# Four output projections stream their 256 tokens in another order of 64- or 128-byte pieces

## The chip, the core and the metric

The kernel runs on one core of one Trainium2 chip. The metric is the device time of one execution in microseconds (us). Three runs of the kernel before took 2223.46, 2226.57 and 2227.17 us; the median is 2226.57.

## What is computed

Three layers of a sequence model are computed for 256 tokens of width 2048, in fp32: an mLSTM and convolution mixer with a gated feed-forward layer, then a gated linear attention (GLA) mixer, then a latent attention (MLA) mixer. Cut to what matters here, four dense layers end the parts of it:

```
h = h + merged @ w_out                          # "wout":   2048 -> 2048
h = h + (silu(gate) * val) @ w_down             # "wdown":  5504 -> 2048
y = (o * silu(gate)) @ l0_gla_w_out             # "glaout": 2048 -> 2048
y = (o * silu(gate)) @ l1_mla_w_out             # "mlaout": 2048 -> 2048
x = x + rms_norm(y, g_post)                     # after glaout and mlaout
```

Before wdown stands the up projection (`hn @ w_up`, 2048 to 2 times 5504), a root-mean-square norm ahead of it.

## The kernel before, in words

Activations lie transposed in the on-chip memory (SBUF): 128 features on the partitions, the 256 tokens along each partition (`T = 256`, four bytes each, so 1024 bytes of a partition to a tile of features). Weights come from DRAM as one stream in the order of their use, in units of 128 x 1024 numbers, four units in a ring. ScalarE rounds each unit to `w_hi` (line 921), VectorE makes the rest `w_lo` (line 1337); each activation is held as a `hi` and a `lo` part too. A product of a 128 x 128 block of weights with a tile of tokens is then three matmuls in `tile` (lines 554 to 556): `w_hi` with `hi`, `w_hi` with `lo`, `w_lo` with `hi`. In each the block of weights is loaded into the array (the stationary operand, row "PEld" of the profile), and the 256 tokens stream past it (the moving operand) and are added in 256 columns of a PSUM bank, `acc0` or `acc1`. `feature_tile` does this for 16 blocks, that is 48 matmuls and two units of weights; wout, glaout and mlaout are 16 such tiles each (768 matmuls each), wdown is 16 tiles of 43 blocks (2064 matmuls), the up projection 86 tiles (4128 matmuls).

`token_tiles` (lines 596 to 598) has the roles the other way round: tokens are stationary, 256 or 512 columns of the weights stream. Sums over features (norms, softmax) and the small products of attention are plain fp32 matmuls, each of which the chip runs as two passes. One of these stands inside the up projection: `norm_sum` (line 605) is issued between the two units of its first tile.

The order on TensorE is fixed by the program: the stages follow each other in one instruction stream, the fixed loops of each stage wait only on semaphores for the next unit (`lo_ready`), for the bank (`acc_taken`) and for their inputs. VectorE and ScalarE read `acc` after the last matmul of a tile, columns 0 to 255 in their natural order.

Where the operands lie is set by the layout: `apart` (192 bytes) stands between the weights and `n_hi`, and the shared area starts 64 bytes past a multiple of 256:

```
LINE = 256
apart = sb("apart", [P, LINE // 4 * 3 // 4])
arena_start = -(-(nc.sbuf_base - LINE // 4) // LINE) * LINE + LINE // 4
```

With this layout every unit of `w_hi` and `w_lo` starts 128 bytes past a multiple of 256, and every tile of a moving operand of `tile` (`n_hi`, `mg_hi`, `f_hi`, `og_hi`, `mo_hi`, `c_hi` and their `lo` parts) starts 64 bytes past one.

Of the kernel before, what the change touches and what calls it, by code (L numbers as in the profile page):

```python
# [19 lines left out]
T = 256  # L20
D = 2048
KT = D // P
# [7 lines left out]
F_TILES = D_FF // P  # L30
# [5 lines left out]
RING = 4  # L36
FREE = 1
LINE = 256


PHASES = [
# [26 lines left out]
def program(nc, x_in, stream_in, params_in, v_bias_in, gk2_in, positions_in, out):  # L68
# [26 lines left out]
    with ctx:  # L95
        def sb(name, shape, dt=fp32):
            return ctx.enter_context(nc.sbuf_tensor(name, shape, dt))
# [15 lines left out]
        w_hi = sb("w_hi", [P, RING, UNIT], fp32r)  # L113
        w_lo = sb("w_lo", [P, RING, UNIT], fp32r)
        apart = sb("apart", [P, LINE // 4 * 3 // 4])
        n_hi = sb("n_hi", [P, KT, T], fp32r)
# [16 lines left out]

        arena_start = -(-(nc.sbuf_base - LINE // 4) // LINE) * LINE + LINE // 4
        arena_end = nc.sbuf_usable_end
# [14 lines left out]
        a = Arena(arena_start)  # L150
# [12 lines left out]
        a = Arena(mixer_temps)  # L163
# [45 lines left out]
        a = Arena(arena_start)  # L209
        f_hi = a.place("f_hi", [P, F_TILES, T], fp32r)  # L210
        f_lo = a.place("f_lo", [P, F_TILES, T], fp32r)
# [11 lines left out]
        a = Arena(arena_start)  # L223
# [24 lines left out]
        a = Arena(y_at)  # L248
        log_a = a.place("log_a", [P, G_HEADS, 2 * T])
        rank_rows = a.place("rank_rows", [32, T])  # L250
        a = Arena((arena_end - 4 * T) // 32 * 32)
        out_rstd = a.place("out_rstd", [P, T])
        a = Arena(y_at + 4 * G_HEADS * 2 * T + 4 * T)
        gk2 = a.place("gk2", [G_RANK + 1, G_HEADS * G_DK])
        a = Arena(y_at)
# [7 lines left out]
        a = Arena(arena_start)  # L263
# [4 lines left out]
        c_hi = a.place("c_hi", [P, 2 * A_TILES, T], fp32r)  # L268
        c_lo = a.place("c_lo", [P, 2 * A_TILES, T], fp32r)
# [14 lines left out]
        a = Arena(y2_at)  # L284
# [5 lines left out]
        a = Arena(y2_at)  # L290
# [7 lines left out]
        a = Arena(arena_start + 4 * 2 * C_TILES * T)  # L298
# [238 lines left out]
        def _(pe):  # L537
            def unit(name, i, j):

                u, s, _ = unit_of(name, i, j)  # L540
                pe.wait_ge(lo_ready, u + 1)
                return s

            def bank(b, name, i, j):

                uses = count(1 + b, name, i, j)
                if i is not None or uses:
                    pe.wait_ge(acc_taken[b], FREE + uses)
                return acc[b]

            def tile(out, s, c, hi, lo, k, first, last):

                wc = slice(c * P, (c + 1) * P)
                nc.tensor.matmul(out, w_hi[:, s, wc], hi[:, k, :], start=first, stop=False)  # L554
                nc.tensor.matmul(out, w_hi[:, s, wc], lo[:, k, :], start=False, stop=False)  # L555
                return nc.tensor.matmul(out, w_lo[:, s, wc], hi[:, k, :], start=False, stop=last)  # L556

            def feature_tile(name, i, j, b, use, hi, lo, wait_act=None, ready=(), unscaled=None, between=None):

                o = bank(b, name, i, use)[:, 0:T]  # L560
                for n in range(2):
                    s = unit(name, i, j + n)
                    for c in range(8):
                        if wait_act is not None and c % 4 == 0:

                            four = wait_act * KT // 4 + 2 * n + c // 4 + 1
                            pe.wait_ge(act_ready, 3 * four)
                            pe.wait_ge(act_ready_dve, four)
                        if unscaled is not None:

                            pe.wait_ge(xlo_ready, UNSCALED[unscaled] * KT + 8 * n + c + 1)
                        if c % 4 == 0:

                            for signal, per in ready:
                                pe.wait_ge(signal, FREE + (8 * n + c + 4) // per)
                        last = tile(o, s, c, hi, lo, 8 * n + c, n + c == 0, 8 * n + c == KT - 1)
                    last.then_inc(unit_done, 1)
                    if n == 0 and between is not None:
                        between()
# [40 lines left out]


            feature_tile("gates", None, 0, 0, 0, n_hi, n_lo, wait_act=0)

            def mix(i):
                feature_tile("mix", i, 0, 1, 0, n_hi, n_lo)
                feature_tile("mix", i, 2, 0, 0, n_hi, n_lo)


# [43 lines left out]
            with pe.Fori(0, KT // 2) as i:  # L672
                for m in range(2):
                    feature_tile("merge", i, 6 * m, 1, 2 * m, n_hi, n_lo)
                    feature_tile("merge", i, 6 * m + 2, 0, 2 * m, n_hi, n_lo)
                    for n, (hi, lo) in enumerate(((hm_hi, hm_lo), (yc_hi, yc_lo))):

                        if n == 0:
                            pe.wait_ge(hmlo_ready, FREE + M_HEADS)
                        else:  # L680
                            pe.wait_ge(yclo_ready, FREE + 2 * M_HEADS)
                        o = bank(1 - n, "merge", i, 2 * m + 1)[:, 0:T]
                        s = unit("merge", i, 6 * m + 4 + n)
                        for c in range(8):
                            last = tile(o, s, c, hi, lo, c, c == 0, c == 7)
                        last.then_inc(unit_done, 1)

            with pe.Fori(0, KT // 2) as i:
# [14 lines left out]
            with pe.Fori(0, KT // 2) as i:  # L703
                for m in range(2):
                    o = bank(1 - m, "wdown", i, 0)[:, 0:T]
                    for n in range(6):
                        s = unit("wdown", i, 6 * m + n)
                        pe.wait_ge(flo_ready, FREE + min(8 * n + 8, F_TILES))
                        for k in range(8 * n, min(8 * n + 8, F_TILES)):
                            last = tile(o, s, k - 8 * n, f_hi, f_lo, k, k == 0, k == F_TILES - 1)  # L710
                        last.then_inc(unit_done, 1)


# [112 lines left out]
            def pair_tile(i, j, b, use, k0):  # L826


                pe.wait_ge(c_ready, k0 + A_TILES)
                o = bank(b, "mla", i, use)  # L830
                s = unit("mla", i, j)
                for c in range(8):
                    m, k = divmod(c, A_TILES)
                    last = tile(o[:, m * T:(m + 1) * T], s, c, c_hi, c_lo, k0 + k, k == 0,
                                k == A_TILES - 1)
                return last

# [30 lines left out]
            with pe.Fori(0, A_HEADS // 4) as i:  # L868
                for n in range(2):
                    pair_tile(i, 2 * n, 0, n, 0).then_inc(unit_done, 1)  # L870
                    pair_tile(i, 2 * n + 1, 1, n, A_TILES).then_inc(unit_done, 1)

                last = pair_tile(i, 4, 0, 2, 0)
                unit("mla", i, 5)
                last.then_inc(unit_done, 2)
# [1361 lines left out]
```

## Time and profile before

| | |
|---|---|
| median of 3 runs | 2226.57 us |
| the profiled execution's own time | 2226.45 us |
| its span, first to last instruction | 2224.7 us |
| TensorE matmul busy | 2145.7 us (96%), 17596 instructions |
| TensorE weight load busy | 2104.9 us (95%) |
| VectorE, ScalarE, GpSimd busy | 59%, 52%, 13% |
| mean granted TensorE clock | 0.985 of 2.4 GHz |
| DMA | 177 GB/s mean, 49% of the 16 engines |

The profile is of one execution. Its matmuls are pipelined and their ends are modelled: one of 256 columns is shown with 276 or 281 ns while the next starts some 115 ns later. So the busy share says little of how fast TensorE goes; the distance from one start to the next (the pitch, below) says it. It is read from the first and the last start of a group and its count, or from the number of matmuls in a stretch. A matmul of line 554, 555 or 556 counts once each.

### The profile page before, as it was taken

The page shows a single profiled execution, that of the slowest core. Times are in us where ns is not written, and L with a number is a line of the kernel's source. Part 1 is how long each engine was busy: PE and PEld are TensorE (multiplying, and loading weights), DVE is VectorE, ACT ScalarE, POOL GpSimd, SP SyncE. Part 2 cuts the span into 40 slices and gives each one's busy share as a digit, 9 for nine tenths or more (in the row PEclk, how much of TensorE's full clock was granted, in tenths as well). Part 3 has the DMA queues.
Part 4 walks back from the last instruction along what each step waited for, and adds up shares of the span by engine and source line. Part 5 has one row for each costly group of instructions (what it writes and reads, how often), then busy time and mean ns, then how long its engine had stood idle before and what let it go on. Part 6 is the DMA issues. An engine that isn't in the chain of part 4 may idle for free.

```text
span 2224.7 us, 46503 instructions
## 1 busy us (share of the span) xinstructions
PE 2145.7 (96%) x17596; PEld 2104.9 (95%) x17596; DVE 1312.7 (59%) x1641; ACT 1158.4 (52%) x1544; POOL 283.3 (13%) x325
## 2 busy tenths in 40 slices
PE   5999999999999999999999999999999979999996
PEld 5999999999999999999999999999998969899996
DVE  5655664544557666666765545655665465755644
ACT  5444545555546555555554444644554445656542
POOL 2000000010110111111111100001010123111112
PEclk8999999999999999999999999999999989999998
DMA  4454545555555555555545555445444434444453
GB/s 150 172 183 174 189 163 198 194 187 202 189 189 192 186 188 189 187 183 181 187 186 208 193 218 212 146 178 190 171 169 170 171 131 147 157 151 152 155 183 113
DMA packets 54927, 393.83 MB, mean 177 GB/s; under 512 B 6097, under 2 KB 6225, under 8 KB 7522
## 3 DMA queue, kind: packets, MB, share of 16 engines
q1 hardware_dynamic: 54432, 392.19, 49.2%
q10 hardware_dynamic: 450, 1.02, 0.1%
q8 instruction: 31, 0.51, 0.1%
q14 instruction: 14, 0.11, 0.0%
HBM read 391.09 MB, written 2.10 MB: 177 GB/s over the span
## 4 chain that ended last, share of the span: by engine, by line
PE 80%; issue 13%; POOL 3%; DVE 2%; ACT 2%; DMA 0%; POOLq 0%; DVEq 0%; ACTq 0%
PE acc L554 23%; PE acc L555 23%; PE acc L556 23%; PE tok L596 2%; PE tok L598 2%; PE tok L597 2%; POOL n_lo L1927 1%; POOL sumsq_g L1918 1%; PE att L614 1%; POOL x L1940 0%; POOL probs L2080 0%; DVE rstd L1345 0%; POOL probs L2077 0%; PE att L788 0%; PE att L864 0%
## 5 line engine op out<-in xcount | busy, mean ns | idle before, releaser
L1337 DVE TENSOR_TENSOR w_lo<-raw,w_hi 128x1024 fp32r<-128x1024 f32 x740 | 907.0, 1239 | 728.2 <-ACT w_hi L921 726.1
L921 ACT ACTIVATE w_hi<-raw 128x1024 fp32r<-128x1024 f32 x740 | 770.0, 1056 | 594.7 <-PE acc L556 363.5
L554 PE MATMUL acc<-n_hi,w_hi 128*128 128x256 f32 x3488 | 986.7, 283 | 26.8 <-POOL n_lo L1927 19.4
L555 PE MATMUL acc<-n_lo,w_hi 128*128 128x256 f32 x3488 | 979.6, 281 | 0.0
L556 PE MATMUL acc<-n_hi,w_lo 128*128 128x256 f32 x3488 | 979.4, 281 | 0.0
L554 PEld LDWEIGHTS acc<-n_hi,w_hi 128*128 128x128 f32 x3488 | 668.7, 192 | 30.1 <-issue 20.2
L555 PEld LDWEIGHTS acc<-n_lo,w_hi 128*128 128x128 f32 x3488 | 662.0, 190 | 0.5
L556 PEld LDWEIGHTS acc<-n_hi,w_lo 128*128 128x128 f32 x3488 | 660.8, 189 | 0.0
L555 PE MATMUL acc<-f_lo,w_hi 128*128 128x256 f32 x688 | 193.5, 281 | 0.0
L556 PE MATMUL acc<-f_hi,w_lo 128*128 128x256 f32 x688 | 193.5, 281 | 0.0
L554 PE MATMUL acc<-f_hi,w_hi 128*128 128x256 f32 x688 | 193.5, 281 | 0.0
L554 PEld LDWEIGHTS acc<-f_hi,w_hi 128*128 128x128 f32 x688 | 132.2, 192 | 0.0
L555 PEld LDWEIGHTS acc<-f_lo,w_hi 128*128 128x128 f32 x688 | 129.2, 188 | 0.0
L556 PEld LDWEIGHTS acc<-f_hi,w_lo 128*128 128x128 f32 x688 | 129.2, 188 | 0.0
L1994 POOL TENSOR_TENSOR f_lo<-f_act,f_hi 128x256 f32 x43 | 57.6, 1340 | 432.3 <-ACT f_hi L1100 432.3
L1916 POOL TENSOR_TENSOR sumsq<-sumsq,square 128x256 f32<-128x256 f32 x64 | 47.3, 739 | 444.4 <-ACT square L930 227.5
L596 PE MATMUL tok<-w_hi,n_hi 128*128 128x256 f32 (+1 forms) x256 | 87.6, 342 | 0.0
L598 PE MATMUL tok<-w_hi,n_lo 128*128 128x256 f32 (+1 forms) x256 | 87.2, 341 | 0.0
L597 PE MATMUL tok<-w_lo,n_hi 128*128 128x256 f32 (+1 forms) x256 | 87.2, 341 | 0.0
L554 PE MATMUL acc<-og_hi,w_hi 128*128 128x256 f32 x256 | 72.1, 282 | 3.1 <-DVE og_lo L1730 3.1
L554 PE MATMUL acc<-mo_hi,w_hi 128*128 128x256 f32 x256 | 72.1, 282 | 0.0
L555 PE MATMUL acc<-mo_lo,w_hi 128*128 128x256 f32 x256 | 72.0, 281 | 0.0
(313 smaller groups left out, 2950.8 us busy)
## 6 DMA issues: line engine op xcount, KB each, us to landing
raw<-stream_in SPq DMA_DIRECT2D x370, 1024.0 KB, 4.8
x<-x_in SPq DMA_DIRECT2D x4, 512.0 KB, 7.4
out<-x SPq DMA_DIRECT2D x4, 512.0 KB, 2.6
v_bias<-v_bias_in ACTq DMA_DIRECT2D x1, 512.0 KB, 8.9
par<-params_in ACTq DMA_DIRECT2D x1, 287.0 KB, 5.5
pos_i<-positions_in ACTq DMA_DIRECT2D x1, 128.0 KB, 6.8
gk<-gk_in ACTq DMA_DIRECT2D x1, 68.0 KB
```

What stands on the lines that cost most here:

```text
L554: nc.tensor.matmul(out, w_hi[:, s, wc], hi[:, k, :], start=first, stop=False)
L555: nc.tensor.matmul(out, w_hi[:, s, wc], lo[:, k, :], start=False, stop=False)
L556: return nc.tensor.matmul(out, w_lo[:, s, wc], hi[:, k, :], start=False, stop=last)
L596: nc.tensor.matmul(o, hi[:, k0 + k, tt], w_hi[:, s, wc], start=k == 0, stop=False)
L597: nc.tensor.matmul(o, hi[:, k0 + k, tt], w_lo[:, s, wc], start=False, stop=False)
L598: last = nc.tensor.matmul(o, lo[:, k0 + k, tt], w_hi[:, s, wc], start=False, stop=k == n_k - 1)
L614: last = nc.tensor.matmul(att[3][:, 0:T], ones[:, :], squares_all[:, k, :], start=k == 0, stop=k == KT - 1)
L921: nc.scalar.activation(w_hi[:, s, :], raw[:, s, :], ACT.Copy).then_inc(hi_ready, 1)
L1337: nc.vector.tensor_tensor(w_lo[:, s, :], raw[:, s, :], w_hi[:, s, :].bitcast(fp32), ALU.subtract).then_inc(lo_ready, 1)
L1916: ins = gp.tensor_tensor(sumsq[:, :], sumsq[:, :], square[:, m, :], ALU.add)
L1918: ins = gp.tensor_tensor(sumsq_g[:, :], sumsq_g[:, :], square_g[:, m, :], ALU.add)
L1994: gp.tensor_tensor(f_lo[:, i, :], f_act[:, :], f_hi[:, i, :].bitcast(fp32), ALU.subtract)\
```

## The change

`tile` is given the name of its stage. For the four output stages it views the token axis of the moving operand and of the PSUM output through the same rearrangement, so each token's result still lands in its own column, while tokens are visited in another order. In units of 64-byte pieces (16 tokens), numbered 0 to 15 along the tile, the orders are:

- wout: 0 2 4 6 8 10 12 14, then 1 3 5 7 9 11 13 15
- wdown: 0 8 1 9 2 10 3 11 4 12 5 13 6 14 7 15
- glaout: 0 1, 8 9, 2 3, 10 11, 4 5, 12 13, 6 7, 14 15
- mlaout: 0 1, 4 5, 8 9, 12 13, then 2 3, 6 7, 10 11, 14 15

All other stages keep the natural order. No instruction is added, removed or moved on any engine; the matmuls of the four stages have one more level in two of their access patterns. Nothing that VectorE, ScalarE, GpSimd or the DMA queues do is changed.

```
+STREAMED = {"wout": "p (a b e) -> p b a e", "wdown": "p (b a e) -> p a b e",
+            "glaout": "p (b a e) -> p a b e", "mlaout": "p (a b e) -> p b a e"}
+STREAM_RUN = {"wout": 16, "wdown": 16, "glaout": 32, "mlaout": 32}
...
-            def tile(out, s, c, hi, lo, k, first, last):
+            def streamed(name, t):
+
+                if name not in STREAMED:
+                    return t
+                return t.rearrange(STREAMED[name], b=2, e=STREAM_RUN[name])
+
+            def tile(name, out, s, c, hi, lo, k, first, last):
 
                 wc = slice(c * P, (c + 1) * P)
-                nc.tensor.matmul(out, w_hi[:, s, wc], hi[:, k, :], start=first, stop=False)
-                nc.tensor.matmul(out, w_hi[:, s, wc], lo[:, k, :], start=False, stop=False)
-                return nc.tensor.matmul(out, w_lo[:, s, wc], hi[:, k, :], start=False, stop=last)
+                out, high, low = streamed(name, out), streamed(name, hi[:, k, :]), streamed(name, lo[:, k, :])
+                nc.tensor.matmul(out, w_hi[:, s, wc], high, start=first, stop=False)
+                nc.tensor.matmul(out, w_hi[:, s, wc], low, start=False, stop=False)
+                return nc.tensor.matmul(out, w_lo[:, s, wc], high, start=False, stop=last)
...
-                        last = tile(o, s, c, hi, lo, 8 * n + c, n + c == 0, 8 * n + c == KT - 1)
+                        last = tile(name, o, s, c, hi, lo, 8 * n + c, n + c == 0, 8 * n + c == KT - 1)
...
-                            last = tile(o, s, k - 8 * n, f_hi, f_lo, k, k == 0, k == F_TILES - 1)
+                            last = tile("wdown", o, s, k - 8 * n, f_hi, f_lo, k, k == 0, k == F_TILES - 1)
```

## Rows read from the trace of the kernel before

**Rows 1.** The page: busy time of the engines, share of the span, instructions
```profile
PE 2145.7 (96%) x17596; PEld 2104.9 (95%) x17596; DVE 1312.7 (59%) x1641; ACT 1158.4 (52%) x1544; POOL 283.3 (13%) x325
```
**Rows 2.** Longest waits of TensorE: in total, times, longest, us
```profile
PE acc L554 <- POOL n_lo L1927: 19.4, 5, 7.7
...
PE acc L554 <- DVE og_lo L1730: 3.1, 1, 3.1
```
**Rows 3.** Matmuls by operand: duration ns min/median/max, first and last start, us
```profile
L554 PE MATMUL acc<-mg_hi,w_hi x256: 275/276/277, 591.5 to 678.2; 128*128 128x256 f32 x128
...
L554 PE MATMUL acc<-f_hi,w_hi x688: 280/281/282, 1165.1 to 1407.8; 128*128 128x256 f32 x172
...
L554 PE MATMUL acc<-og_hi,w_hi x256: 280/281/356, 1713.7 to 1807.1; 128*128 128x256 f32 x128
...
L554 PE MATMUL acc<-mo_hi,w_hi x256: 280/281/363, 2114.7 to 2204.8; 128*128 128x256 f32 x128
```
**Rows 4.** Stretches, us: length, busy and count per engine, clock, DMA share, GB/s
```profile
400.00:560.00 160.00, 160.00 (x1415) 160.00 (x1414) 80.02 (x80) 83.81 (x98) 13.47 (x19) 1.00 0.54 195
...
700.00:1100.00 400.00, 400.00 (x3398) 400.00 (x3398) 277.54 (x389) 228.85 (x301) 48.75 (x36) 1.00 0.52 186
```
**Rows 5.** Timeline of TensorE around the norm's sum: start, duration us, instruction
```profile
680.24 0.28 PE L554 MATMUL acc<-n_hi,w_hi 128*128 128x256 f32 x1
...
681.15 0.28 PE L556 MATMUL acc<-n_hi,w_lo 128*128 128x256 f32 x1
681.26 0.59 PE L605 MATMUL att<-sumsq,ones 128*128 128x256 f32 x2
681.51 0.47 PE L554 MATMUL acc<-n_hi,w_hi 128*128 128x256 f32 x1
...
682.05 0.28 PE L554 MATMUL acc<-n_hi,w_hi 128*128 128x256 f32 x1
...
687.70 0.28 PE L554 MATMUL acc<-n_hi,w_hi 128*128 128x256 f32 x1
```
**Rows 6.** Timeline: last 256-column and first 512-column matmuls, MLA, third pass
```profile
2019.60 0.28 PE L554 MATMUL acc<-c_hi,w_hi 128*128 128x256 f32 x1
...
2020.28 0.39 PE L596 MATMUL tok<-w_hi,c_hi 128*128 128x512 f32 x1
...
2025.09 0.39 PE L596 MATMUL tok<-w_hi,c_hi 128*128 128x512 f32 x1
```
**Rows 7.** The same, MLA, fourth pass
```profile
2073.86 0.28 PE L554 MATMUL acc<-c_hi,w_hi 128*128 128x256 f32 x1
...
2074.57 0.40 PE L596 MATMUL tok<-w_hi,c_hi 128*128 128x512 f32 x1
...
2079.47 0.40 PE L596 MATMUL tok<-w_hi,c_hi 128*128 128x512 f32 x1
```
**Rows 8.** Timeline: plain fp32 matmuls, two passes each ("x2")
```profile
147.39 0.38 PE L653 MATMUL att<-weighted,vm 128*128 128x128 f32 x2
147.61 0.60 PE L652 MATMUL att<-weighted,vm 128*128 128x256 f32 x2
```
**Rows 9.** Weight loads and matmuls of wdown by line, as in rows 3
```profile
L554 PEld LDWEIGHTS acc<-f_hi,w_hi x688: 191/192/193, 1164.9 to 1407.7; 128*128 128x128 f32 x172
...
L556 PEld LDWEIGHTS acc<-f_hi,w_lo x688: 187/188/188, 1165.2 to 1407.9; 128*128 128x128 f32 x172
```
**Rows 10.** Around the sums after wdown: timeline of TensorE
```profile
1407.79 0.28 PE L554 MATMUL acc<-f_hi,w_hi 128*128 128x256 f32 x1
...
1410.62 0.28 PE L554 MATMUL acc<-n_hi,w_hi 128*128 128x256 f32 x1
...
1411.37 0.70 PE L717 MATMUL att<-sumsq,ones 128*128 128x256 f32 x2 [0.24 <-POOL sumsq_g L1918]
...
1413.48 0.28 PE L554 MATMUL acc<-n_hi,w_hi 128*128 128x256 f32 x1
...
1417.90 0.28 PE L554 MATMUL acc<-n_hi,w_hi 128*128 128x256 f32 x1
```

More of the change, by code:

```diff
@@ L684, in _ @@
                         for c in range(8):
-                            last = tile(o, s, c, hi, lo, c, c == 0, c == 7)
+                            last = tile("merge", o, s, c, hi, lo, c, c == 0, c == 7)
                         last.then_inc(unit_done, 1)
@@ L833, in pair_tile @@
                     m, k = divmod(c, A_TILES)
-                    last = tile(o[:, m * T:(m + 1) * T], s, c, c_hi, c_lo, k0 + k, k == 0,
+                    last = tile("mla", o[:, m * T:(m + 1) * T], s, c, c_hi, c_lo, k0 + k, k == 0,
                                 k == A_TILES - 1)
```

## The prediction

> **What bounds the kernel now.** I read four views, in this order. First the busy shares: TensorE has a matmul in flight for 2145.7 of 2224.7 us, VectorE is at 59% and ScalarE at 52% [rows 1]. The reader is to see that nothing but TensorE is near its limit, and that 96% cannot tell how fast it goes, since the ends of matmuls are modelled. Second, TensorE's waits: the longest group adds up to 19.4 us in 5 waits, and the only one that touches one of the four output stages is 3.1 us, once, at the head of glaout [rows 2]. So those stages have no slack to find: their length is their number of matmuls times the pitch from start to start.
>
> Third, the pitch by stage [rows 3]. wout runs from 591.5 to 678.2 us, 255 blocks of three matmuls: 86.7 / 765 = 113.3 ns. wdown: 242.7 / (687 x 3 = 2061) = 117.8 ns. mlaout: 90.1 / 765 = 117.8 ns. glaout: 93.4 less the 3.1 of the wait, / 765 = 118.0 ns. These are the same instructions, 256 columns, the same clock, and yet two pitches, which the shown durations mark too: 276 ns at the short pitch, 281 at the long. They are levels and not a drift: 400 to 560 us, in merge, is all at the short one (160 us / 1415 = 113.1, a little low because one already running at the edge is counted) and 700 to 1100, in the up projection, all at the long one (400 / 3398 = 117.7), both at a granted clock of 1.00 [rows 4].
>
> Fourth, what changes the level. Before `norm_sum` the pitch is 0.91 us for 8 matmuls, 113.8 ns; behind its two passes it is 5.65 us / 48 = 117.7 ns, in one and the same loop with the same operands [rows 5]. After wdown the reverse: 2.83 / 24 = 117.9 ns across the end of wdown into the rank tile, then three plain fp32 sums, then 4.42 / 39 = 113.3 ns [rows 10]. The stream keeps its level until something breaks its rhythm, also across a change of stage. I call them the short and the long lock.
>
> **What the difference hangs on.** In the MLA passes a run of 512-column matmuls follows a run of 256 without a gap. Behind a short run (0.68 / 6 = 113.3 ns) the 512s take 4.81 / 21 = 229.0 ns [rows 6]; behind a long one (0.71 / 6 = 118.3) they take 4.90 / 21 = 233.3 ns [rows 7]. The difference is 4.3 to 4.5 ns a matmul at both widths. So it is not paid by column but once per matmul, and each matmul has one weight load beside it. The loads show it as well: in wdown those of line 554 take 192 ns where those of line 556 take 188 [rows 9]. I read this as two streams out of one memory, tokens at twice the pace of weights, that meet in two possible ways. What the change alters is which addresses the fast stream has when the slow one has its own.
>
> **The change part by part.**
>
> *Instructions.* None added, removed or moved; 4368 matmuls (768 + 2064 + 768 + 768) get another access pattern in the moving operand and in PSUM. The readers of `acc` and the DMA queues have the same work. VectorE and ScalarE, at 59% and 52%, have the room to follow a TensorE that is 4% faster in these stages. So every nanosecond of pitch goes to the end of the kernel at full price.
>
> *wdown, glaout, mlaout.* All three stand at the long lock. No row shows a 256-column stream in pieces, so the new pitch is bounded from its nearest rows. Below: plain fp32 passes of 128 columns stream at half the rate in the same time, and two of them with their weight loads take 147.61 - 147.39 = 0.22 us, 110 ns each [rows 8]; 256 / 2.4 = 106.7 ns is what the columns alone take at the granted clock. So 110 ns is what a pitch without meetings could be. Above: 233.3 - 117.8 = 115.5 ns is paid for 256 more columns, 8.9 more than the clock needs, or 2.2 ns for each of the four 256-byte stretches of a 1024-byte row. If that price belongs to entering a 256-byte stretch, pieces cost more (rival C). Between 110 and some 142 the nearest measured values are the two locks themselves, and I take the short one, 113.3: with the order of pieces changed, the tokens no longer sweep past the weights in one direction, and the long way of meeting loses its footing. Worth: 2064 x 4.45 ns = 9.2 us in wdown, 768 x 4.45 = 3.4 us each in glaout and mlaout, 16.0 us together.
>
> *wout.* It is at 113.3 now, and I leave it there: 0. Its bounds are (113.3 - 110) x 768 = 2.5 us of gain and one lock, 3.4 us, of loss.
>
> *What comes behind wout.* The up projection has 4128 matmuls, 24 of them ahead of `norm_sum`; 4104 x 4.45 ns = 18.3 us lie between its two locks. Which one it gets is decided by how the stream stands when `norm_sum` breaks it, and the new order of wout may shift that. It stands at the long lock now, so this can only gain. I take 0, because its own matmuls and the sum are unchanged, and keep 18.3 us for the lower end.
>
> *Sum.* 2226.45 (the profiled execution; 1.75 us of it lie outside the span) - 16.0 = 2210.4 us. The profiled execution is 0.1 us below the median of the runs, so no correction.
>
> A rule of the skill bears on the pieces. The rows show two pitches for one access pattern and none for another [rows 3]. The Trainium skill, "SBUF — State Buffer", section "Who interferes with whom", says that TensorE reads moving operand and weights through two independent ports and never waits on anyone; "TensorE: Matmul & The Clock Gate", section "Back-to-back issue gap", gives 256 / 2.4 + 2.5 = 109.2 ns as the gap (an estimate by that page). By these the order of the tokens could not matter, and both stages would already run at 109; the trace has 113.3 and 117.8, so something else is paid here, and rival A is what is left of the rule.
>
> **The rivals.**
>
> *A. The order does not matter.* The price is in the loads or in the count of columns, the locks are set by the plain sums between the stages, and these are untouched. For it: the lock survives a change of operand tile and stage [rows 10], and wout and merge share a lock though their tiles are others. Against: nothing in the rows, since no other order was ever run. Time: 2226.45, within 2225 to 2228.
>
> *B. The up projection changes its lock too,* or wdown runs near 110. 2210.4 - 18.3 = 2192.1; with wdown at 110 instead of 113.3, 2210.4 - 6.8 = 2203.6. For it: rows 5, a lock decided by one small event. Against: it has to fall the right way.
>
> *C. Entering a 256-byte stretch is what costs (slower).* With tiles starting 64 bytes past a multiple of 256, the natural order enters a new stretch 4 times; the new orders do 8 (wout), 15 (wdown), 11 (glaout) and 8 times (mlaout). At 2.2 ns: 4 x 2.2 x 768 = 6.8, 11 x 2.2 x 2064 = 50, 7 x 2.2 x 768 = 11.8 and 6.8 us, 75 in all: 2302 us. A mild form is one step of 4.45 ns more in each of the 4368 matmuls, 19.4 us: 2245.9. For it: the 8.9 ns that wider matmuls pay beyond the clock, with or without a lock [rows 6, 7]. Against: the plain fp32 matmuls show nothing of the kind, though they go at half the rate. It decides from where the mean pitch of the four stages passes 117.0 ns, what they have now ((113.3 x 768 + 117.8 x 3600) / 4368); each ns above is 4.4 us.
>
> A rule of the skill speaks for C. The Trainium skill, "Advanced Engine Details and Errata", section "Memory Cachelines", says that any non-contiguous access pattern in PSUM significantly slows down matmuls, and in the same place that every two consecutive elements should be contiguous. By its first sentence all four stages would be slower, by its second none, since the shortest piece here has 16 elements. No row of this trace shows a broken pattern in PSUM.
>
> **How the numbers follow.** The forecast as it stands, 16 us faster give or take some of the stages: 0.32. B, more than that: 0.15. A: 0.18. C: 0.35, of which 0.20 for the mild form (2231 to 2250) and 0.15 for the full one. A measurement of this kernel can tell 0.2%, 4.5 us, from no change. Faster by more than that: 0.32 + 0.15, with 0.01 for a single stage gaining = 0.48. Within it: 0.17. Slower: 0.35. The forecast's own range is 2205 to 2221 (one of the smaller stages not following, or wout gaining too). The range that holds 8 in 10 goes from B's 2192, with a little of wdown's other gain (2188), to the end of C's mild form, 2250; left out are most of the full form and a small part of B.
>
> **What would show it.** The median duration shown for matmuls on f_hi, og_hi and mo_hi: 276 ns if they took the short lock, 281 if nothing changed, above if C holds, nearer 272 if the meetings are gone. First and last start of f_hi: 687 x 3 x 113.3 ns = 233.6 us against 242.7 now. The count of matmuls in 400 us of the up projection: 3398 now, 3530 at the short lock. The pitch on either side of `norm_sum` tells whether wout hands on another lock. If the four stages turn out with four pitches, the order matters and my single step is too coarse; if wdown alone is above 125 ns, the forecast is wrong and C stands. If the four stages do not change and the time does, the locks of the other stages moved.

## The result: slower by 0.6%, in the four stages that were changed

| | before | changed |
|---|---|---|
| median of 4 runs | 2226.87 us | 2240.58 us |
| ratio, 95% interval | 1 | 1.006, 1.0047 to 1.0073 |
| profiled execution | 2226.45 us | 2241.23 us |
| its span | 2224.7 us | 2239.5 us |

The page's line of busy time shows nothing but a little more of TensorE, and the same instructions; it answers to [rows 1]:

```profile
PE 2162.1 (97%) x17596; PEld 2120.2 (95%) x17596; DVE 1313.9 (59%) x1641; ACT 1159.6 (52%) x1544; POOL 282.7 (13%) x325
```

The first matmuls of the blocks of the four stages, by operand (duration min/median/max, first and last start), answer to [rows 3]:

```profile
L564 PE MATMUL acc<-mg_hi,w_hi x256: 282/285/288, 592.0 to 684.8; 128*128 128x256 f32 x128
...
L564 PE MATMUL acc<-f_hi,w_hi x688: 281/283/284, 1171.7 to 1419.0; 128*128 128x256 f32 x172
...
L564 PE MATMUL acc<-og_hi,w_hi x256: 278/282/416, 1723.9 to 1819.6; 128*128 128x256 f32 x128
...
L564 PE MATMUL acc<-mo_hi,w_hi x256: 280/283/366, 2127.8 to 2219.6; 128*128 128x256 f32 x128
```

Subtract first from last start. wout takes 92.8 us (86.7 before), wdown 247.3 (242.7), glaout 95.7 (93.4), mlaout 91.8 (90.1): 6.1 + 4.6 + 2.3 + 1.7 = 14.7 us, against 14.8 in the span. What lies ahead of wout and between the stages moved too, by 0.5 to 1.0 us either way, and comes to nothing in sum. The pitches are 92.8 / 765 = 121.3 ns, 247.3 / 2061 = 120.0, and 91.8 / 765 = 120.0. glaout's is read from a stretch without its wait; here are stretches of the changed kernel (length, busy and count per engine, clock, DMA share, GB/s), in the order up projection, wdown, glaout, mlaout, wout:

```profile
700.00:1100.00 400.00, 400.00 (x3399) 400.00 (x3398) 277.12 (x390) 228.87 (x301) 47.35 (x35) 1.00 0.52 186
1200.00:1400.00 200.00, 200.00 (x1669) 200.00 (x1668) 102.01 (x105) 93.17 (x116) 18.59 (x26) 1.00 0.55 202
1745.00:1815.00 70.00, 70.00 (x592) 70.00 (x591) 33.34 (x37) 32.28 (x50) 8.95 (x13) 1.00 0.52 182
2140.00:2210.00 70.00, 70.00 (x586) 70.00 (x585) 28.33 (x24) 32.62 (x51) 9.54 (x13) 1.00 0.49 178
600.00:680.00 80.00, 80.00 (x662) 80.00 (x661) 44.53 (x56) 36.78 (x54) 9.59 (x14) 1.00 0.48 175
```

The count includes two matmuls already running at the edge, so glaout's pitch is 70 / 590 = 118.7 (118.8 from start to start). It grew by 1.5 us more than its pitch says. TensorE waits 3.1 us at the head of the stage; from 1732.6 to 1735.8 us, a microsecond after that wait, matmuls start 0.21 us apart, and the granted clock is 0.50 (1.2 GHz):

```profile
1733.00:1735.00 2.00, 2.00 (x12) 2.00 (x11) 0.00 (x0) 1.41 (x3) 0.73 (x1) 0.50 0.03 8
```

That belongs to the clock and not to the order: the same fall stands behind the same wait in e2, e3, e14 and e15 below, where glaout has the natural order, and is missing in e11, where it has a new one. The up projection has 3399 matmuls in its 400 us where it had 3398 [rows 4]: the same long lock.

Behind wout the stream falls back at once. In this timeline of the changed kernel the reader is to see 24 matmuls of the up projection at (687.91 - 685.18) / 24 = 113.8 ns, with the first three, still near 120, among them; then the sum, then 118 ns, as in [rows 5]:

```profile
684.82 0.28 PE L564 MATMUL acc<-mg_hi,w_hi 128*128 128x256 f32 x1
...
685.18 0.28 PE L564 MATMUL acc<-n_hi,w_hi 128*128 128x256 f32 x1
...
687.91 0.59 PE L615 MATMUL att<-sumsq,ones 128*128 128x256 f32 x2
688.16 0.47 PE L564 MATMUL acc<-n_hi,w_hi 128*128 128x256 f32 x1
...
688.58 0.28 PE L566 MATMUL acc<-n_hi,w_lo 128*128 128x256 f32 x1
688.70 0.28 PE L564 MATMUL acc<-n_hi,w_hi 128*128 128x256 f32 x1
688.82 0.28 PE L565 MATMUL acc<-n_lo,w_hi 128*128 128x256 f32 x1
```

So each new order has a pitch of its own, the same from the first tile to the last, and leaves no trace behind its stage in this trace. (In e8 and e13 below the stream left wout on the long lock instead.)

### The profile page after: what moved, and what is told of

The parts are those of the page before. It is cut to its first block, busy times and chain, and to the rows that moved or that the text cites. A ratio compares the mean times of both kernels' runs of the same rounds, so it can differ in the third digit from the quotient of the medians.

```text
span 2239.5 us, 46503 instructions
## 1 busy us (share of the span) xinstructions
PE 2162.1 (97%) x17596; PEld 2120.2 (95%) x17596; DVE 1313.9 (59%) x1641; ACT 1159.6 (52%) x1544; POOL 282.7 (13%) x325
## 4 chain that ended last, share of the span: by engine, by line
PE 80%; issue 13%; POOL 3%; DVE 2%; ACT 2%; DMA 0%; POOLq 0%; DVEq 0%; ACTq 0%
PE acc L564 23%; PE acc L565 23%; PE acc L566 23%; PE tok L606 2%; PE tok L608 2%; PE tok L607 2%; POOL n_lo L1937 1%; POOL sumsq_g L1928 1%; PE att L624 0%; POOL x L1950 0%; POOL probs L2090 0%; DVE rstd L1355 0%; POOL probs L2087 0%; PE att L798 0%; PE att L874 0%
## 5 line engine op out<-in xcount | busy, mean ns | idle before, releaser
L566 PE MATMUL acc<-mg_hi,w_lo 128*128 128x256 f32 x256 | 72.9, 285 | 0.0
L565 PE MATMUL acc<-mg_lo,w_hi 128*128 128x256 f32 x256 | 72.9, 285 | 0.0
```

The lines of the kernel that those rows point to most:

```text
L565: nc.tensor.matmul(out, w_hi[:, s, wc], low, start=False, stop=False)
L566: return nc.tensor.matmul(out, w_lo[:, s, wc], high, start=False, stop=last)
```

## The experiments

The theories. **M**: tokens and weight loads meet in memory, by their place modulo 256 bytes. **J** (also called S where it is about natural order): the moving stream pays by itself, for jumps or for stretches entered, whatever the loads do. **R** and **W**: the price is on the reading or on the writing side. All pitches in this table are means over the steady part of a stage, worked out from the starts in each trace. Times are of single executions, with that of the kernel before on the same chip beside them; those of e15 and e16 are medians of 4, and 2224.05 is a median of 7 that lie between 2219.78 and 2226.01. So a time of one execution tells less than the pitches do. The up projection is not in the table: behind `norm_sum` it ran at 113.3 ns in e3, e8, e12, e15 and e16 (18.3 us less) and at 117.8 in all others.

| run | us (before beside it) | wout | wdown | glaout | mlaout |
|---|---|---|---|---|---|
| before | 2226.45 | 113.3 | 117.8 | 117.8 | 117.8 |
| changed | 2241.23 | 121.3 | 120.0 | 118.8 | 120.0 |
| e1 read only | 2240.37 (2224.76) | 121.3 | 120.0 | 118.8 | 120.0 |
| e2 write only | 2225.65 (2224.76) | 113.3 | 117.8 | 113.3 | 117.8 |
| e3 sum twice | 2200.04 (2224.76) | 113.3 | 113.3 | 113.3 | 117.8 |
| e4 tokens moved 64 bytes | 2247.32 (2224.76) | 120.0 | 120.0 | 120.0 | 120.0 |
| e5 all moved 64 bytes | 2221.07 (2228.73) | 113.3 | 117.8 | 113.3 | 117.8 |
| e6 changed, tokens at 0 | 2256.42 (2228.73) | 120.0 | 123.3 | 120.0 | 120.0 |
| e7 changed, tokens at 192 | 2239.32 (2228.73) | 120.0 | 120.0 | 120.0 | 120.0 |
| e8 changed, half loads | 2224.04 (2228.73) | 120.0 | 120.7 | 120.0 | 117.8 |
| e9 natural, half loads | 2234.61 (2224.62) | 113.3 | 119.0 | 119.0 | 119.0 |
| e10 other orders | 2232.48 (2224.62) | 113.3 | 117.8 | 116.7 | 123.3 |
| e11 orders swapped | 2238.84 (2224.62) | 118.8 | 121.3 | 120.0 | 120.0 |
| e12 changed, sum twice | 2225.90 (2224.62) | 121.3 | 120.0 | 118.8 | 120.0 |
| e13 loads moved 64 bytes | 2240.20 (2224.05) | 120.0 | 120.0 | 120.0 | 120.0 |
| e14 sum three times | 2226.96 (2224.05) | 113.3 | 117.8 | 113.3 | 117.8 |
| e15 e3 again, timed | 2200.61 (2224.05) | 113.3 | 113.3 | 113.3 | 117.8 |
| e16 toggled | 2192.99 (2224.05) | 113.3 | 113.3 | 113.3 | 113.3 |

### Reading or writing (e1, e2)

```
-out, high, low = streamed(name, out), streamed(name, hi[:, k, :]), streamed(name, lo[:, k, :])
+high, low = streamed(name, hi[:, k, :]), streamed(name, lo[:, k, :])              # e1
+out, high, low = streamed(name, out), hi[:, k, :], lo[:, k, :]                    # e2
```

> The changed kernel, but the output in PSUM is written in natural order: only the moving operand is read in the new order (so the columns of the four stages hold other tokens' sums). Theory R (the order costs on the reading side, in SBUF): the four stages keep the changed kernel's pitches, 121.3, 120.0, 118.8 and 120.0 ns (wout, wdown, glaout, mlaout), time 2240. Theory W (it costs on the writing side, in PSUM): they go back to 113.3 or 117.8, time 2227 or less.

> The changed kernel, but the moving operand is read in natural order: only the PSUM columns are written in the new order (columns again hold other tokens' sums). Theory R: 113.3 in wout and 117.8 in the other three, time 2227. Theory W: the changed kernel's four pitches, time 2240.

e1 has the changed kernel's four pitches, e2 the two locks of natural order. The steady stages of e2 by operand:

```profile
L564 PE MATMUL acc<-mg_hi,w_hi x256: 276/276/276, 590.1 to 676.8; 128*128 128x256 f32 x128
...
L564 PE MATMUL acc<-f_hi,w_hi x688: 281/281/281, 1163.7 to 1406.4; 128*128 128x256 f32 x172
```

Writing PSUM in pieces of 64 or 128 bytes costs nothing that can be seen; the whole price is on the side where tokens are read. glaout took the short lock in e2, as in e3, e5, e14, e15 and e16; of the traces in which it reads in natural order, with whole loads and tokens 64 bytes ahead of them, only that of the kernel before has it at 117.8. Behind its wait the landing differs, so 117.8 is not a fixed mark for glaout.

### The place modulo 256 (e4, e5, e6, e7)

```
-arena_start = -(-(nc.sbuf_base - LINE // 4) // LINE) * LINE + LINE // 4
+arena_start = -(-(nc.sbuf_base - 128) // LINE) * LINE + 128     # e4, and e5
+shifted = sb("shifted", [P, 16])                                # e5 alone, ahead of x
+arena_start = -(-(nc.sbuf_base - 0) // LINE) * LINE + 0         # e6, with the change
+arena_start = -(-(nc.sbuf_base - 192) // LINE) * LINE + 192     # e7, with the change
```

> The kernel before, natural order, with the shared area moved by 64 bytes: moving operands of the four stages then start at the same place modulo 256 as the weights (128 past a multiple) instead of 64 bytes ahead of it; n_hi stays. Theory M (tokens and weights meet in memory, by address modulo 256): the pitches of wout, wdown, glaout and mlaout become others than 113.3 and 117.8, while the up projection, whose operands lie as before, shows only those two; a rise of up to 9 ns, at most +39 us. Theory S (the moving stream pays by itself, for each stretch it enters): start 128 past a multiple still enters four new stretches, so the two pitches stay.

> The kernel before, natural order, with 64 bytes put ahead of everything: weights start 192, all tiles of tokens 128 bytes past a multiple of 256. Theory M (what counts is where tokens lie relative to weights, modulo 256): as the kernel before, 113.3 and 117.8 ns, time 2227. Theory S (what counts is where the moving stream itself starts, as 128 in the run with the shared area moved): 120.0 in all four output stages, time about 2247 or more, the up projection too.

> The changed kernel's four orders with the shared area moved so that the moving operands of the four stages start at a multiple of 256, 128 bytes ahead of the weights' place instead of 64. Theory M: the four pitches change, and not all the same way; wdown's order keeps pace with the weights and could then stay clear of them, 110 to 113 ns, 14 to 20 us less in that stage. Theory J (each jump of the stream costs, wherever it lies): 121.3, 120.0, 118.8 and 120.0 stay within 0.5 ns, time 2240.

> As the run before, but with the moving operands of the four stages 192 bytes past a multiple of 256, 64 bytes behind the weights' place. Theory M: again other pitches than 121.3, 120.0, 118.8 and 120.0, some up and some down. Theory J: they stay.

e4 and e5 have the output stages' tokens at the same place, 128 past a multiple of 256, in natural order. In e4 the weights are at 128 too, in e5 at 192. The up projection and wdown of e4, then of e5:

```profile
700.00:1100.00 400.00, 400.00 (x3399) 400.00 (x3398) 277.79 (x390) 229.85 (x302) 47.30 (x35) 1.00 0.52 186
1200.00:1400.00 200.00, 200.00 (x1669) 200.00 (x1668) 102.04 (x104) 94.15 (x117) 18.71 (x26) 1.00 0.56 203
```
```profile
700.00:1100.00 400.00, 400.00 (x3399) 400.00 (x3398) 276.99 (x390) 229.61 (x302) 48.14 (x36) 1.00 0.52 185
1200.00:1400.00 200.00, 200.00 (x1701) 200.00 (x1700) 104.16 (x107) 94.32 (x118) 18.71 (x26) 1.00 0.57 207
```

1669 against 1701 matmuls in 200 us is 120.0 against 117.8 ns. What counts is where tokens lie relative to something else that e5 moved along. In e4 merge shows it too, within one stage: 1389 matmuls start in its 160 us where 1415 did, because `hm_hi` and `yc_hi`, which lie in the moved area, go at 120.0 and `n_hi` between them, which does not, at 113.4. e6 and e7 say the same of the new orders: their pitches are not the orders' own but belong to an order at a place. They also say that 128 bytes would be too short a period: e7 and the changed kernel have their tokens 128 bytes apart and differ in wout (120.0 and 121.3) and glaout (120.0 and 118.8). wdown's order, which I had hoped would keep clear of the weights once shifted, is worst there: 123.3. No shift brought one of the four orders under 118.8.

### Are the weight loads what is met? (e13, e8, e9)

```
 if name in STREAMED:
+    at = c * P - 16 if c else 48
+    wc = slice(at, at + P)                 # e13, tokens in natural order
...
+    wc = slice(c * P, c * P + 64)          # e8 with the new orders, e9 in natural order
+    out = out[0:64]
```

> The kernel before, natural order, tokens where they were (64 bytes past a multiple of 256), but in the four stages each weight load begins 64 bytes earlier modulo 256 (16 columns earlier, the first block of a unit 48 later), so that it takes other columns of the unit than it should; nothing else is moved. Loads and tokens then start at the same place modulo 256, as in the run with the shared area moved by 64 bytes. If the weight loads are what the tokens meet: 120.0 ns in wout, wdown, glaout and mlaout as there, time about 2247. If it was another buffer's place: 113.3 and 117.8 stay, time 2227.

> The changed kernel, but the four stages load only 64 of the 128 weight columns of each block and write 64 rows of PSUM (half of each output tile is left out); the moving streams are the same. Theory M: with half the weight reads there are half the meetings, the part of the pitch above some 109 ns halves, 121.3, 120.0, 118.8, 120.0 become about 115, 114.5, 114 and 114.5. Theory J: the moving stream is as it was and the pitches stay.

> The kernel before in natural order, with only 64 of 128 weight columns loaded per block in the four stages (half of each output tile left out). Pair to the run with half loads and the new orders, which stayed at 117.8 to 120.6. Theory M (meetings with the weight loads are what is paid): 110 to 112 ns in the four stages. Theory J (the moving stream pays by itself): 113.3 or 117.8 as with whole loads. If natural order falls and the new orders did not, what the new orders pay is not paid to the loads alone.

e13 moves no buffer at all, only the address at which a load of the four stages begins. Its stretches, in the order merge, wout, up projection, wdown, glaout, mlaout (merge and the up projection load as before):

```profile
400.00:560.00 160.00, 160.00 (x1414) 160.00 (x1414) 80.69 (x79) 84.91 (x98) 13.29 (x18) 1.00 0.54 192
610.00:680.00 70.00, 70.00 (x586) 70.00 (x585) 38.60 (x49) 32.93 (x50) 8.90 (x12) 1.00 0.52 182
700.00:1100.00 400.00, 400.00 (x3398) 400.00 (x3397) 277.26 (x390) 228.65 (x300) 47.71 (x35) 1.00 0.53 186
1200.00:1400.00 200.00, 200.00 (x1669) 200.00 (x1669) 101.86 (x104) 93.22 (x117) 18.71 (x26) 1.00 0.55 203
1745.00:1815.00 70.00, 70.00 (x585) 70.00 (x585) 33.08 (x36) 32.00 (x49) 8.91 (x12) 1.00 0.51 181
2140.00:2210.00 70.00, 70.00 (x586) 70.00 (x585) 28.87 (x25) 32.62 (x50) 8.89 (x12) 1.00 0.49 172
```

All four stages go to 120.0 ns (their counts are those of e4 within one), while merge and the up projection stay. So the counterpart is the weight load: shown, by moving it alone. The expected time, 2247, was too high for that reason, since in e4 the merge stage and others paid too. e13 is in natural order; for the new orders e8 says that the loads matter, since with the same token streams all four pitches changed (121.3, 120.0, 118.8, 120.0 became 120.0, 120.7, 120.0, 117.8).

How the price comes about is not shown. Half the columns per load should have halved the meetings, and did not: e9 kept 113.3 in wout and rose to 119.0 in the others, e8 stayed between 117.8 and 120.7. Weight loads and matmuls of wdown in e9:

```profile
L567 PEld LDWEIGHTS acc<-f_hi,w_hi x688: 133/134/138, 1164.2 to 1409.5; 128*64 128x64 f32 x172
L567 PE MATMUL acc<-f_hi,w_hi x688: 278/281/285, 1164.3 to 1409.6; 128*64 128x256 f32 x172
```

The load is shown 54 ns shorter than [rows 9] have it, and the matmuls start 245.3 / 2061 = 119.0 ns apart. So neither theory in its simple form holds: not a price for each byte loaded, and not a price that ignores the loads. And since a load half as long leaves the best pitch at 113.3, the length of the load is not what sets 113.3 either.

### Is a jump paid, and does the stage matter? (e10, e11)

```
+STREAMED = {"wout": "p (b a e) -> p a b e", "wdown": "p (b a e) -> p a b e",
+            "glaout": "p (a b e) -> p b a e", "mlaout": "p (b a e) -> p a b e"}     # e10
+STREAM_RUN = {"wout": 64, "wdown": 64, "glaout": 8, "mlaout": 8}
...
+STREAMED = {"wout": "p (b a e) -> p a b e", "wdown": "p (a b e) -> p b a e",
+            "glaout": "p (a b e) -> p b a e", "mlaout": "p (b a e) -> p a b e"}     # e11
+STREAM_RUN = {"wout": 32, "wdown": 16, "glaout": 32, "mlaout": 16}
```

> Other orders in the four stages. wout and wdown: pieces of 256 bytes in the order 0 2 1 3, so the stream jumps three times but its addresses modulo 256 are those of the natural order. glaout: 32-byte pieces, even ones then odd ones; mlaout: 32-byte pieces taken from the two halves in turn; 31 jumps each. Theory M (only the place modulo 256 against the weights counts): wout and wdown at 113.3 or 117.8. Theory J (a jump costs): wout and wdown 1 to 3 ns above their lock, glaout and mlaout clearly above 122.

> The changed kernel with its orders dealt otherwise: wout has glaout's, wdown has wout's, glaout has mlaout's, mlaout has wdown's. If the order alone sets the pitch: 118.8, 121.3, 120.0, 120.0 ns, and the time (121.3 in the longest stage) about 2240.6 - 1.9 + 2.8 = 2241. If the stage (its entry, its operands) sets it: 121.3, 120.0, 118.8, 120.0 as in the changed kernel.

In e10 wout and wdown jump (256-byte pieces in the order 0 2 1 3) but read the same addresses modulo 256 as natural order. wout, wdown, glaout and mlaout of e10:

```profile
610.00:670.00 60.00, 60.00 (x531) 60.00 (x531) 35.24 (x46) 29.92 (x44) 8.15 (x11) 1.00 0.55 192
1200.00:1400.00 200.00, 200.00 (x1701) 200.00 (x1700) 102.53 (x105) 93.45 (x117) 18.74 (x26) 1.00 0.57 210
1740.00:1800.00 60.00, 60.00 (x517) 60.00 (x516) 30.73 (x34) 27.96 (x42) 7.43 (x11) 1.00 0.52 187
2130.00:2200.00 70.00, 70.00 (x569) 70.00 (x569) 28.32 (x24) 30.68 (x48) 8.08 (x11) 1.00 0.48 171
```

The two locks of natural order are back in full: 113.3 and 117.8 (1701 in 200 us, as in e5). A jump over whole multiples of 256 bytes costs nothing here, which speaks for the sequence of places modulo 256. Two orders of 32-byte pieces with 31 jumps each have 116.7 and 123.3 ns: theory J is out a second time. 116.7 is the one new order seen below the long lock; none reached 113.3.

e11 deals the same orders to other stages, and each order takes its pitch along: 118.8 to wout, 121.3 to wdown, 120.0 to the two others (these two cannot be told apart, both orders had 120.0 before). The stage, its operands and the lock from which it is entered do not matter.

### What sets the lock (e3, e14, e12)

```
 if n == "ffn":
+    nc.tensor.matmul(att[3][:, 0:T], ones[:, :], sumsq[:, :], start=True, stop=True)   # once more (e3, e12), twice more (e14)
```

> The kernel before, with the matmul of the norm's sum inside the up projection issued twice (two passes more, 0.43 us). Theory of the toggle (each such sum moves the stream from one lock to the other): up projection and wdown at 113.3 instead of 117.8, 4104 + 2064 matmuls x 4.45 ns = 27 us less, time 2200. Theory of the fixed landing (the sum always leaves the long lock, whatever stood before): 117.8 as before, time 2227.

> The kernel before with the norm's sum in the up projection issued three times. Toggle: odd number, so the long lock again, up projection and wdown at 117.8, time 2227 + 0.9. If it was the longer break and not the number that helped with two: 113.3 and 2201.

> The changed kernel with the norm's sum inside the up projection issued twice. If the toggle works there as in the kernel before: up projection at 113.3, 18.3 us less. wdown is then entered from the short lock: if its order has one pitch only, 120.0 stays and the time is 2222; if the order has two locks as the natural one has, wdown goes 4.45 ns down to some 115.6, 9 us less again, 2213.

With the sum issued twice the up projection and wdown run at the short lock from end to end. The timeline around the two sums and the two stages' stretches, from the timed run of this kernel (e15):

```profile
680.18 0.28 PE L556 MATMUL acc<-n_hi,w_lo 128*128 128x256 f32 x1
680.29 0.59 PE L606 MATMUL att<-sumsq,ones 128*128 128x256 f32 x2
680.72 0.59 PE L607 MATMUL att<-sumsq,ones 128*128 128x256 f32 x2
680.97 0.47 PE L554 MATMUL acc<-n_hi,w_hi 128*128 128x256 f32 x1
```
```profile
700.00:1100.00 400.00, 400.00 (x3532) 400.00 (x3531) 287.11 (x406) 237.97 (x312) 49.49 (x37) 1.00 0.54 193
1160.00:1360.00 200.00, 200.00 (x1767) 200.00 (x1766) 107.00 (x110) 99.47 (x124) 20.10 (x28) 1.00 0.59 214
```

3532 matmuls where there were 3398. With three sums it is the long lock again. The up projection of e14:

```profile
700.00:1100.00 400.00, 400.00 (x3399) 400.00 (x3398) 277.14 (x389) 228.86 (x302) 48.69 (x36) 1.00 0.52 186
```

At this place, from the short lock, one sum leads to long (11 traces), two to short (e3, e12, e15, e16), three to long (e14), so a longer break is not better by itself. Whether the number decides, or how long the break is, is not separated: each sum also adds 0.43 us. The rule does not reach further than that. From the long lock the landing is not as plain: in e13 the sum came upon the long lock and left the long one, in e8 upon the long and left the short. And the three sums behind wdown, with a wait of 0.2 to 0.3 us among them, lead from the long lock to the short in the kernel before [rows 10] but leave the long one in e14, 0.11 to 0.12 us from start to start:

```profile
1411.64 0.70 PE L720 MATMUL att<-sumsq,ones 128*128 128x256 f32 x2 [0.25 <-POOL sumsq_g L1921]
...
1413.16 0.28 PE L555 MATMUL acc<-n_lo,w_hi 128*128 128x256 f32 x1
...
1421.41 0.28 PE L556 MATMUL acc<-n_hi,w_lo 128*128 128x256 f32 x1
```

These are 70 matmuls in 8.25 us, 117.9 ns. From the short lock the same three sums led to the short in e15 and to the long in e16.

e12 puts the same double sum into the changed kernel. Up projection and wdown of e12:

```profile
700.00:1100.00 400.00, 400.00 (x3532) 400.00 (x3531) 287.50 (x406) 238.38 (x313) 50.31 (x37) 1.00 0.54 193
1160.00:1360.00 200.00, 200.00 (x1669) 200.00 (x1669) 102.08 (x104) 94.08 (x117) 18.61 (x26) 1.00 0.55 200
```

The up projection gains as it should, and wdown, now entered from the short lock, stays at 120.0. So wdown's order shows one pitch from either lock; natural order has two, and 120.0 is worse than both.

### A version that beats both (e15, e16)

```
+    nc.tensor.matmul(att[3][:, 0:T], ones[:, :], o_sum[:, :], start=True, stop=True)   # GLA, ahead of the same one
...
+pe.wait_ge(tok_taken, FREE + 2 * count(3, "mla", A_HEADS // 4, 0))                     # ahead of mlaout
+nc.tensor.matmul(tok[0][:, 0:T], ones[:, :], sine[:, :], start=True, stop=True)
```

> The kernel with the norm's sum issued twice, timed: 27 us of pitch less 0.4 us for two passes more, 2200, ratio to before 0.988.

> Natural order, norm's sum in the up projection twice; each head's sum in GLA (o_sum) twice, four times in all; and one plain fp32 matmul of constants ahead of mlaout. If each toggles: the up projection and wdown short (27 us); three whole and one short run behind the GLA sums short (3 x 237 and 80 matmuls, 3.5 us, less 1.7 for the passes, and glaout may flip either way, 3.4); mlaout short (3.4 less 0.4). Time 2194 to 2200. If the toggle fails where waits stand between, mlaout stays at 117.8 and the time is 2200.

e15, the double sum alone: 2200.61 us (median of 4) against 2224.05, ratio 0.990 (0.988 to 0.991). e16, with the added matmuls in GLA and ahead of mlaout: 2192.99 us, ratio 0.987 (0.985 to 0.988). Both compute the same results as before with a few matmuls more. In the trace of e15 the stretch from `norm_sum` to the end of wdown is 27 us shorter, as expected; the medians differ by 23.4 us. Where the other 3.6 us went the runs do not show. The up projection of e16 has the 3532 matmuls of e15. A stretch of 256-column matmuls behind a sum in GLA in e16 and, for comparison, in e15, then mlaout in e16:

```profile
1541.00:1561.00 20.00, 20.00 (x179) 20.00 (x179) 15.46 (x25) 13.29 (x16) 1.30 (x1) 1.00 0.45 178
1540.00:1560.00 20.00, 20.00 (x172) 20.00 (x171) 15.47 (x26) 13.01 (x15) 1.30 (x1) 1.00 0.48 176
2100.00:2160.00 60.00, 60.00 (x532) 60.00 (x531) 26.13 (x23) 29.29 (x45) 8.14 (x11) 1.00 0.49 179
```

All four output stages are at 113.3. An added matmul moved the lock at each of the three kinds of place: in the up projection, behind the GLA sums (179 matmuls in 20 us instead of 172) and ahead of mlaout, which is at 117.8 in the six other traces in natural order (before, e2, e3, e5, e14, e15) and at 113.3 in this one. glaout does not count for it, it is at 113.3 in e15 as well.

## Why the prediction was wrong, point by point

**What bounds the kernel: right.** TensorE has no slack in the four stages, and the change of their length came out at the end at full price: 14.7 of 14.8 us.

**The failed step: the pitch of the new orders.** "Between 110 and some 142 the nearest measured values are the two locks themselves, and I take the short one, 113.3: with the order of pieces changed ... the long way of meeting loses its footing." The long way did lose its footing, and so did the short: each order got one pitch, 118.8 to 121.3, above both locks. The sign that was named for it did show: the median durations on f_hi, og_hi and mo_hi are 283, 282 and 283 ns, above the 281 of the long lock. In the terms of the sum: wdown -9.2 was +4.6; glaout -3.4 was +0.8, and 1.5 more from the clock; mlaout -3.4 was +1.7; wout 0 was +6.1. The largest error for a stage's size is wout, which stood at the short lock: I bounded its loss at "one lock, 3.4 us", and it lost 8.0 ns a matmul, 6.1 us. glaout's +0.8 is small by luck: the kernel before happened to have it at 117.8, and against the 113.3 of the other runs in natural order it would be +4.2. Nothing in the rows made 113.3 the nearest value rather than 117.8. I chose the side; the bounds of 110 and 142 held.

**The reading that tokens and loads meet: right that the load's place counts,** which e13 shows. That they collide in the memory stays a picture; half the load did not halve the price (e9). "Each matmul has one weight load beside it" and a difference that does not grow with the width were enough to find it. But from "they meet" I concluded which order would meet less, without one row that gave the price of any other relation. The wish that wdown's order, keeping pace with the weights, would avoid them is refuted at three places: 120.0, 123.3 and 120.0 ns.

**The up projection's lock: 0 came true, the reason given for it does not hold.** In the changed kernel the stream leaves wout's order within three matmuls for the short lock, and `norm_sum` then lands where it did. But in e8 and e13 wout left the stream on the long lock, and in e8 the same single sum then led to the short one, 18.3 us less, with the up projection's "own matmuls and the sum" unchanged. The 18.3 us were there to be had, by another cause (e15: 23.4 us with wdown's share).

**Rival A, the order does not matter: refuted.** With it falls, for this case, what the Trainium skill, "SBUF — State Buffer", section "Who interferes with whom", says of TensorE's two read ports, that they are independent: the measurement is 113.3 or 117.8 against 120.0 ns for loads that begin 64 bytes elsewhere. The 109.2 ns was read too widely in the prediction: the Trainium skill, "TensorE: Matmul & The Clock Gate", section "Back-to-back issue gap", gives it for an isolated matmul and says that in a stream of loads and matmuls both set the spacing. No run here came to it.

**Rival B, the up projection changes its lock too or wdown runs near 110: did not come.** No run shows any stage of 256 columns under 113.3.

**Rival C, slower: right in sign, wrong in mechanism.** Its mild form gave 2245.9 for a step of 4.45 ns in each matmul; the mean step was 13.2 us / 4368 = 3.0 ns. But what it named, entering a 256-byte stretch, is not paid: e10 enters more stretches than natural order and keeps its pitches, and the count of entries (8, 15, 11, 8) does not rank the four pitches (121.3, 120.0, 118.8, 120.0). The Trainium skill, "Advanced Engine Details and Errata", section "Memory Cachelines", would have the loss in PSUM by its first sentence and none by its second; e2 agrees with the second: 113.3 and 117.8 ns, 2225.65 against 2224.76 us.

**The range held the time, the sign was missed.** The range of 2188 to 2250 took in the mild form of C, and 2240.6 lies in it.

## What to carry to other kernels

When the same matmuls run at two pitches in one profile, look for what stands between the two stretches before touching operands: here one plain fp32 matmul, issued once more, was worth 23.4 us, and the reordering of a quarter of all matmuls cost 13.7. Such a gain has to be looked for by trial, since no rule found here foretells every landing. A placement that has been found to run well holds for one relation of two streams; changing the order of one of them gives that up, and "they will meet otherwise" is no reason to expect less. If a kernel has several stages of one kind, giving each another variant shows in a single profile what each variant costs, as the changed kernel did.

## What the runs showed of the hardware that was not expected

- Two locks of one instruction stream, 113.3 and 117.8 ns, each kept for thousands of matmuls (6168 in e3: 4104 of the up projection and 2064 of wdown) until a break or a stage with another order or place comes. From the short lock one, two and three two-pass fp32 sums inside the up projection led to long, short and long; from the long lock, and behind wdown, where a wait stands in the break, the landing differed between runs.
- The pitch depends on the place of the token stream relative to the weight load modulo 256 bytes: in natural order tokens 64 bytes ahead of the load's place give 113.3 or 117.8; at the same place 120.0. Other places were not run in natural order.
- The order of the pieces changes the pitch: 120.0 to 123.3 ns with pieces of 64 bytes, 118.8 and 120.0 with 128, 116.7 and 123.3 with 32; whole 256-byte pieces in another order do not change it, and pieces of 64 or 128 bytes in PSUM cost nothing.
- A load of 64 columns instead of 128 went with 119.0 in the three stages that had or could have the long lock and left 113.3 in wout. By what the two reads share a resource, and why the steps are what they are, stays open.
